# A gather and matmul stage: 704 gathered value columns, and dense value rows in pairs of blocks from block 32

## The reference

```python
    # xt: (256, 2048); idx, gate: (256, 8 heads, 16 experts); U, Vt: (16384, 2048)
        u = U[ib]
        hid = jax.nn.gelu(jnp.einsum('td,thkd->thk', xb, u))
        v = Vt[ib]
        return jnp.einsum('thk,thkd->td', gb * hid, v)
    x = x + peer_layer(h2, ...)
    return rms_norm(x, norm_f_g)
```

## Time and profile before

| | |
|---|---|
| median of 3 runs | 2129.06 us (2127.1 to 2131.72) |
| the profiled execution: time | 2132.88 us |
| its span, first to last instruction | 2131.1 us |
| mean granted clock of PE | 0.841 of full |
| value stage, about | 1612 to 2117 us of the span |
| PE busy | 1480.5 us (69%) |
| DVE busy | 1619.7 us (76%) |
| ACT busy | 872.1 us (41%) |
| POOL busy | 969.6 us (46%) |

### The profile page before, as it was taken

The page is one execution under the profiler, slowest core; times in us unless marked ns, Lnnn a source line. Parts: engine busy times, 40 slices in busy tenths (PEclk is TensorE's granted clock), DMA queues, the critical chain, the costliest instruction groups (busy, mean ns, idle before and its releaser), DMA issues.

```text
span 2131.1 us, 26457 instructions
## 1 busy us (share of the span) xinstructions
PE 1480.5 (69%) x9809; PEld 1371.6 (64%) x9809; DVE 1619.7 (76%) x2122; ACT 872.1 (41%) x1116; POOL 969.6 (46%) x699
## 2 busy tenths in 40 slices
PE   6999999999999999910000002211358999999997
PEld 6987998898999889910000002211347999999996
DVE  5465764545644556789999999877888999899997
ACT  4354432344333444211211226577655444444443
POOL 1002220000000000178888878888866776667763
PEclk9999999999999999965555555555589999999998
DMA  5555344434455554699999999999917999999996
GB/s 202 177 178 194 139 139 138 153 135 158 158 178 178 198 178 167 250 361 422 421 422 408 416 369 411 412 421 417 419 52 263 357 358 358 350 358 359 359 358 229
DMA packets 151818, 597.85 MB, mean 281 GB/s; under 512 B 14720, under 2 KB 14736, under 8 KB 118288
## 3 DMA queue, kind: packets, MB, share of 16 engines
q0 software_dynamic: 58048, 356.02, 42.0%
q1 hardware_dynamic: 93648, 240.22, 32.0%
HBM read 594.09 MB, written 2.10 MB: 280 GB/s over the span
## 4 chain that ended last, share of the span: by engine, by line
PE 47%; issue 20%; POOL 13%; DVE 13%; DMA 5%; ACT 1%; POOLq 0%; DVEq 0%; SPq 0%; ACTq 0%; PEldq 0%
PE acc L1608 8%; PE acc L1611 8%; PE acc L1610 8%; POOL slots L495 6%; POOL starts L534 5%; DVE slots L1397 5%; PE acc L1625 3%; PE acc L1627 3%; PE acc L1626 3%; DMA starts<-in_v_gather,expert 2%; DMA slots<-in_peer_u,expert 2%; PE acc L1922 2%; PE scr L1924 2%; PE acc L1924 2%; PE scr L1922 2%
## 5 line engine op out<-in xcount | busy, mean ns | idle before, releaser
L881 DVE TENSOR_TENSOR w_lo<-raw,w_hi 128x2048 fp32r<-128x2048 f32 x136 | 314.7, 2315 | 302.8 <-ACT w_hi L550 301.8
L1397 DVE SCALAR_TENSOR_TENSOR slots<-slots,acc 128x2048 f32<-128x2048 f32 x188 | 424.7, 2285 | 46.6 <-DMA slots<-in_peer_u,expert 44.4
L550 ACT ACTIVATE w_hi<-raw 128x2048 fp32r<-128x2048 f32 x136 | 260.1, 1913 | 428.7 <-PE acc L1611 286.5
L534 POOL DMA_INDIRECT starts<-in_v_gather,expert x256 | 343.8, 1343 | 158.9 <-issue 81.3
L495 POOL DMA_INDIRECT slots<-in_peer_u,expert x256 | 250.9, 980 | 260.6 <-DVE expert L1369 148.4
L1608 PE MATMUL acc<-hT_hi,w_hi 128*128 128x256 f32 x1024 | 294.6, 288 | 3.0 <-PE acc L1611 1.7
L503 POOL TENSOR_TENSOR slots<-slots,N 128x2048 f32<-128x2048 f32 x62 | 280.7, 4528 | 31.5 <-DMA slots<-in_peer_u,expert 31.2
L843 ACT ACTIVATE v_hi<-v_raw 128x1408 fp32r<-128x1408 f32 x128 | 177.0, 1384 | 284.3 <-PE scr L1924 213.1
L1610 PE MATMUL acc<-hT_lo,w_hi 128*128 128x256 f32 x1024 | 292.1, 285 | 0.0
L1611 PE MATMUL acc<-hT_hi,w_lo 128*128 128x256 f32 x1024 | 291.9, 285 | 0.0
L746 ACT ACTIVATE slots<-slots 128x2048 f32<-128x2048 f32 x62 | 118.4, 1910 | 366.7 <-POOL slots L503 366.7
(11 more groups left out here) (284 smaller groups left out, 3341.9 us busy)
## 6 DMA issues: line engine op xcount, KB each, us to landing
raw<-in_w_in SPq DMA_DIRECT2D x88, 1024.0 KB
v_raw<-in_v_dense SPq DMA_DIRECT2D x128, 704.0 KB
raw<-in_w_o SPq DMA_DIRECT2D x16, 1024.0 KB
raw<-in_peer_wq SPq DMA_DIRECT2D x16, 1024.0 KB
raw<-in_w_a_up SPq DMA_DIRECT2D x8, 1024.0 KB
raw<-in_w_b_up SPq DMA_DIRECT2D x8, 1024.0 KB
slots<-in_peer_u,expert POOLq DMA_INDIRECT x256, 9.2
starts<-in_v_gather,expert POOLq DMA_INDIRECT x256
```

The source lines that it names most:

```text
L534: pool.indirect_dma_start(starts[s % CRING][:, :], None, v_gather[:, :], bass.IndirectOffsetOnAxis(ap=expert[:, s // NSEL, s % NSEL:s % NS ...
L550: a.activation(w_hi[:, m % 2, :, :], raw[:, m % 2, :, :], ACT.Copy).then_inc(hi_ready, 1)
L881: v.tensor_tensor(w_lo[:, m % 2, :, :], raw[:, m % 2, :, :], w_hi[:, m % 2, :, :].bitcast(fp32), ALU.subtract).then_inc(lo_ready, 1)
L1397: v.scalar_tensor_tensor(out=slots[j][:, :], in0=slots[j][:, :], scalar=1.0, in1=row, op0=ALU.mult, op1=ALU.mult, accum_out=hid_sum[:, t, ...
```

## The change

CW goes from 640 to 704, so that gathers fetch 2816 B a row and the dense part has 1344 columns. Blocks 0 to 31 keep their form (halves of 768 and 576 columns, pieces of 512, 256, 256 and 320). From block 32 (PAIRED_FROM) on:

- SP loads two blocks with one DMA into one of three buffers `v_pair`, 128 x 2688 each. The first lies on SBUF space that `weight_of` for blocks 0 to 31 occupies, the third on that of two `v_raw` buffers; their loads wait accordingly. From the fourth pair on, a load waits until the low parts of the pair that held the buffer are made.
- DVE makes the low part of a block in one operation of 1344 columns, into one of two `v_lo` buffers, waiting for PE to be through with the block before the last (at block 32: with the last). Its two adds follow directly.
- PE waits for a whole block and does tile 0, then tile 1, each in three pieces of 512, 512 and 320 columns.

The core of the diff:

```diff
-CW = 640
+CW = 704
+VBANKS = ((0, 512), (512, 1024), (1024, DW))
+PAIRED_FROM = 32
+PAIRS = 3
@@ buffers
+        v_pair = [at(f"v_pair{j}", kib, [2, DW]) for j, kib in enumerate((24, 34.5, 112))]
-        v_hi, v_lo = at("v_hi", 184, [2, DW], f32r), at("v_lo", 160, [DW], f32r)
+        v_hi = at("v_hi", 184, [2, DW], f32r)
+        v_lo = [at(f"v_lo{n}", kib, [DW], f32r) for n, kib in enumerate((160, 105))]
@@ SP
+            for n in range(PAIRED_FROM, BLOCKS, 2):
+                j = (n - PAIRED_FROM) // 2
+                if j == 0:
+                    sp.wait_ge(e_ready, PAIRED_FROM // 2)
+                elif j == PAIRS - 1:
+                    sp.wait_ge(v_ready, 2 * PAIRED_FROM)
+                elif j >= PAIRS:
+                    sp.wait_ge(v_ready, 2 * (n - 2 * PAIRS) + 4)
+                sp.sem_inc(granted_w, 1)
+                sp.dma_start(v_pair[j % PAIRS][:, :, :], v_dense[:, n:n + 2, :]).then_inc(pair_landed[j % PAIRS], 16)
@@ DVE
+                else:
+                    if n == PAIRED_FROM:
+                        dve.wait_ge(v_used, 2 * n)
+                    elif n > PAIRED_FROM + 1:
+                        dve.wait_ge(v_used, 2 * (n - 2) + 2)
+                    v.tensor_tensor(v_lo[n % 2][:, :], raw_of(n)[:, :], v_hi[:, n % 2, :].bitcast(fp32),
+                                    ALU.subtract).then_inc(v_ready, 2)
+                    add_start(2 * n)
+                    add_start(2 * n + 1)
@@ DVE, after the last block
-                dve.wait_ge(first_done if t == 0 else v_used, 1 if t == 0 else 2 * BLOCKS)
+                dve.wait_ge(v_used, 2 * BLOCKS - 1 + t)
@@ PE
+                else:
+                    pe.wait_ge(v_ready, 2 * n + 2)
                     for t in range(NT):
+                        add(t, VBANKS, v_lo[n % 2]).then_inc(v_used, 1)
```

More of the change, by code:

```diff
@@ L240, in build @@
                      [weight_of1[:, q * P // PIECES:(q + 1) * P // PIECES, :] for q in range(PIECES)]]
-        v_raw = [at(f"v_raw{n}", kib, [DW]) for n, kib in enumerate((112, 117.5, 105))]
-        v_hi, v_lo = at("v_hi", 184, [2, DW], f32r), at("v_lo", 160, [DW], f32r)
+        v_raw = [at(f"v_raw{n}", kib, [DW]) for n, kib in enumerate((112, 117.25, 105))]
+        v_pair = [at(f"v_pair{j}", kib, [2, DW]) for j, kib in enumerate((24, 34.5, 112))]
+        v_hi = at("v_hi", 184, [2, DW], f32r)
+        v_lo = [at(f"v_lo{n}", kib, [DW], f32r) for n, kib in enumerate((160, 105))]
         e_hi, e_lo = at("e_hi", 97, [2, NT, 2 * P], f32r), at("e_lo", 101, [2, NT, 2 * P], f32r)
@@ L245, in build @@
         y_first = at("y_first", 128, [NT, CW])
-        starts = [at(f"starts{n}", kib, [CW]) for n, kib in enumerate((123, 125.5, 195, 197.5, 165.5))]
+        starts = [at(f"starts{n}", kib, [CW]) for n, kib in enumerate((122.5, 125.25, 194.5, 197.25, 165.25))]
         ff_room = at("ff_room", 200, [2 * KB])
@@ L355, in build, with raw_of @@
         v_landed = [sem(f"v_landed{j}") for j in range(RAWS)]
+        pair_landed = [sem(f"pair_landed{j}") for j in range(PAIRS)]
         e_hi_ready, e_ready, v_hi_ready, v_ready, v_used = (
             sem("e_hi_ready"), sem("e_ready"), sem("v_hi_ready"), sem("v_ready"), sem("v_used"))
-        first_done, first_gained, first_out = sem("first_done"), sem("first_gained"), sem("first_out")
+        first_gained, first_out = sem("first_gained"), sem("first_out")
         y_summed, y_ready, out_done = sem("y_summed"), sem("y_ready"), sem("out_done")
+        def raw_of(n):
+            return v_raw[n % RAWS] if n < PAIRED_FROM else v_pair[(n - PAIRED_FROM) // 2 % PAIRS][:, n % 2, :]
         block = ctx.enter_context(nc.Block())
@@ L411, in _ @@
             load_v(2)
-            for n in range(RAWS, BLOCKS):
+            for n in range(RAWS, PAIRED_FROM):
                 sp.wait_ge(v_ready, 2 * (n - RAWS) + 2)
@@ L839, in _ @@
             for n in range(BLOCKS):
-                act.wait_ge(v_landed[n % RAWS], 16 * (n // RAWS + 1))
+                if n < PAIRED_FROM:
+                    act.wait_ge(v_landed[n % RAWS], 16 * (n // RAWS + 1))
+                else:
+                    j = (n - PAIRED_FROM) // 2
+                    act.wait_ge(pair_landed[j % PAIRS], 16 * (j // PAIRS + 1))
                 if n >= 2:
                     act.wait_ge(v_used, 2 * (n - 2) + 2)
-                a.activation(v_hi[:, n % 2, :], v_raw[n % RAWS][:, :], ACT.Copy).then_inc(v_hi_ready, 1)
+                a.activation(v_hi[:, n % 2, :], raw_of(n)[:, :], ACT.Copy).then_inc(v_hi_ready, 1)
                 if n % 2 and n + 1 < BLOCKS:
@@ L1550, in _ @@
                 dve.wait_ge(v_hi_ready, n + 1)
[L1551 to L1556, removed]
+                if n < PAIRED_FROM:
+                    for c, cols in enumerate(VHALF):
+                        if n:
+                            dve.wait_ge(v_used, 2 * (n - 1) + c + 1)
+                        v.tensor_tensor(v_lo[0][:, cols], raw_of(n)[:, cols], v_hi[:, n % 2, cols].bitcast(fp32),
+                                        ALU.subtract).then_inc(v_ready, 1)
+                        add_start(2 * n + c)
+                else:
[7 more added lines that the diff above has]
+                    add_start(2 * n + 1)
                 if n % 2 and n + 1 < BLOCKS:
@@ L1913, in _, with add @@
                 e_cols = slice(n % 2 * P, (n % 2 + 1) * P)
-                for c in range(2):
-                    pe.wait_ge(v_ready, 2 * n + c + 1)
-                    for t in range(NT):
[L1917 to L1928, removed]
+                def add(t, pieces, low):
+                    flat = (acc, scr)[t][:, :, :].rearrange("p a n -> p (a n)")
+                    eh, el = e_hi[:, n // 2 % 2, t, e_cols], e_lo[:, n // 2 % 2, t, e_cols]
+                    for at0, end in pieces:
+                        to, cols = flat[:, at0:end], slice(at0, end)
+                        clear, stop = n == 0 and at0 % GW == 0, n == BLOCKS - 1
+                        t_.matmul(to, eh, v_hi[:, n % 2, cols], start=clear, stop=False, skip_group_check=True)
+                        t_.matmul(to, eh, low[:, cols], start=False, stop=False, skip_group_check=True)
+                        last = t_.matmul(to, el, v_hi[:, n % 2, cols], start=False, stop=stop, skip_group_check=True)
+                    return last
@@ L1931 @@
+                if n < PAIRED_FROM:
+                    for c in range(2):
+                        pe.wait_ge(v_ready, 2 * n + c + 1)
+                        for t in range(NT):
+                            last = add(t, VPIECES[c], v_lo[0])
+                        last.then_inc(v_used, 1)
+                else:
+                    pe.wait_ge(v_ready, 2 * n + 2)
+                    for t in range(NT):
+                        add(t, VBANKS, v_lo[n % 2]).then_inc(v_used, 1)
 _INS = ["x", "norm1_g", "w_in", "fox_f_bias", "hg_lb_logits", "hg_norm_g", "w_a_up", "w_b_up", "w_o", "norm2_g",
```

## The result

The changed kernel took 2152.55 us (median of 4 runs, 2150.45 to 2158.9) beside 2130.39 us for the kernel before (4 runs). The ratio is 1.0106, 95% interval 1.0085 to 1.0127: slower by 22 us. The forecast was 2135 us, range 2108 to 2149.

What follows compares the result with a forecast made beforehand. The prediction took PE to set the pace, at 3.86 us a block, with transfers just fast enough. Terms -4.8 + 8.6 + 3.3 - 1.0 = +6.1 us on a 2129.1 us median gave 2135 us, range 2108 to 2149.

Steps and rivals of the forecast that it cites:

- PE and DVE floors: From block 32, work per block without waits: PE 3.67 us, DVE 3.69 us, so a floor of about 3.68 us.
- Blocks 0 to 31: Fewer dense columns cut PE from 3.86 to 3.68 us a block; with a few adds waiting, -4.8 us.
- The gather ring: From block 32, bunched adds leave gathers less time to land; period 3.95 instead of 3.86 us over 96 blocks, +8.6 us.
- 2P = 0.76 + landing: From block 32, period P per block follows from a gather's landing time, counted from POOL's start; 7.15 us gives 3.95.
- the right side: The whole change was forecast slower, +6.1 us; chances were slower 0.46, same 0.20, faster 0.34.
- meeting a pair in flight: Gather packets each wait behind one longer dense packet; 0.2 us added to a usual landing.
- The seam: At block 32 the first pair's load waits for the low weights of blocks 30 and 31, idling PE: +3.3 us.
- The tail: In the last block DVE adds tile 0 under tile 1's 9 matmuls: -1.0 us.
- In time: Rival: gathers land within 6.6 us, so PE and DVE set 3.68 us a block; -19.8 us, 2109 us, chance 0.34.
- Rate as the bound: Rival: a transfer ceiling of 358 GB/s makes every block need 3.94 us; 2141 us, chance 0.06.

Runs made afterwards that it cites:

- run 9: 704 columns, single loads, seven gather and five dense buffers, plus two low buffers in halves from block 32: 2113.52 us, ratio 0.991 to the kernel before.
- run 2: The changed kernel with each pair loaded by two DMAs issued together, packets of 5376 B instead of 10752 B: 2149.73 us, ratio 1.0082 to the kernel before.
- run 11: The changed kernel with its six blocks of dense buffers each loaded by its own DMA once free: 2140.31 us, ratio 1.0036 to the kernel before.
- run 4: The changed kernel with single-block loads into three buffers, whole low parts and two adds together kept: 2135.85 us, ratio 1.0014 to the kernel before.
- Run 6: The changed kernel with a sixth gather buffer from gather 75 on: 2134.75 us, ratio 1.0006 to the kernel before.
- runs 1 and 6 to 9: Run 6, run 9 and three with 704 columns, single loads: five gather buffers, 2128.9 us; seven, 2122.44 us; seven plus five dense buffers, 2119.17 us.
- run 3: The changed kernel, pair loads kept, with low parts in halves and an add behind each: 2168.0 us, ratio 1.0174 to the kernel before.

## Why the prediction was wrong in size

*PE and DVE floors: right.* PE was to take 3.67 us for a block in three pieces and took 3.64 (1757.29 less 0.17 us of wait, from 1753.48); fewer matmuls brought nothing of their own.

```profile
1753.48 0.39 PE L1955 MATMUL acc<-v_hi,e_hi 128*128 128x512 f32 x1
...
1757.29 0.47 PE L1955 MATMUL acc<-v_hi,e_hi 128*128 128x512 f32 x1
```

DVE's two adds together are 2.00 us long, so the first steps 1.05 us where I had 0.98; its floor is 1.47 + 1.05 + 0.87 + 0.34 = 3.73 us instead of 3.69.

*Blocks 0 to 31: half.* -4.8 us was the term, about -2.4 came. Over the first blocks DVE and PE share one low buffer and take turns in waiting for each other, 3.77 us a block instead of 3.68; run 9, with two buffers, took some of that away later in the stage.

*The gather ring: the right term, mis-sized.* "[...] a usual landing which I put at 6.85, just at the quickest late one: 7.15 us, P = (0.76 + 7.15)/2 = 3.95" is the step that failed. The term was 8.6 us and measured 17.2. By the formula 2P = 0.76 + landing, the measured 4.123 us a block ask for a landing of 7.49 us where I had 7.15.

Two errors of opposite sign stand in that term. The pace after was forecast at 3.95 and is 4.123, over 96 blocks 16.6 us too low. The pace before was taken as PE's 3.86, but is 3.938 in this stretch with its waits, some 7.5 us too low over 96 blocks. Against 3.938 the forecast pace of 3.95 would have meant +1 us and the whole sum no change; that the forecast had the right side is in part luck.

The formula also uses one landing for all gathers, while the late ones cost the time. The trace has lost some of the semaphore updates that tell of landings; from those it kept, 12 of 16 a gather in the mean (14 before), I estimate a median landing of 7.1 us (6.6 before), and 8.7 us or more for one gather in ten (7.5 before). So the usual landing was near what I had put; its spread is what I left out. Of the 383.5 us from block 34 to 127, 347 are DVE's work, 93 x 3.73, 30.2 its waits for gathers, and the rest other waits. Checked at one place the formula is 3% off: with the gather of 7.52 us it gives 8.28 us for two blocks, where the pattern above took 8.03. I had allowed 0.2 us for meeting a pair in flight, reasoning on one dense packet ahead of each gather packet. What the runs show in its place: with short packets in the same burst (run 2) little of the loss is gone. With the same bytes, depth and compute form but single loads (run 11) two thirds of it are gone in time, 3.1 of 12.0 us of that at the seam, but the waits for gathers only fall from 30.2 to 27.3 us; with three blocks ahead instead of six (run 4) they fall to 22.0. So both the 1344 KB asked for at once and the larger amount asked for ahead seem to make gathers late; how much is due to each stays open. Run 6 shows from the other side that late gathers carry the loss.

The Trainium skill's rule from "DMA: Bandwidth & Descriptors" (queues, rings and completion order), that an engine finishes a packet before it turns to another queue, pointed to packet length; by run 2 its share is about 0.24% of the 1.06%, and by the intervals between nothing and half. The trace does not show how an engine chooses, nor whether the packets of that rule are the rows counted here, so why the pair loads hurt more than their packets stays open.

*The seam: right in kind.* 2.69 us of PE idle at block 32 where 3.3 were forecast; its timeline has

```profile
1736.69 0.31 PE L1957 MATMUL scr<-v_hi,e_lo 128*128 128x320 f32 x1
1739.69 0.76 PE L1955 MATMUL acc<-v_hi,e_hi 128*128 128x512 f32 x1 [2.69 <-DVE v_lo L1587]
```

but block 33's second add then waited 1.77 us for a gather (1745.56 above), behind two pairs requested at once; all in all 4.5 us. This wait was not in my sum; that the two pairs made that gather late is inferred from the order of the requests, and no run shows it by itself.

*The tail: wrong sign.* -1.0 us forecast, +0.3 measured. The second add starts at 2138.11, 1.2 us after the last matmul's start (2136.87), where before it was 1.4 (2118.15 and 2116.78): the add of tile 0 is queued behind the gain of the first columns, which waits for ACT's squares (2135.84), and so gets no cover from tile 1's matmuls. I had not looked at what stands ahead of it.

*Rivals.* "In time" did not come about in the changed kernel. Run 9 reaches 19 us under the kernel before, where 19.8 were forecast for that case, but with single loads, seven gather buffers and another form on DVE and PE, so the near number is a coincidence. "Rate as the bound" at 358 GB/s is refuted: 365 to 373 GB/s held for 350 us in runs 1 and 6 to 9. The Trainium skill, in the specifications of "DMA: Bandwidth & Descriptors", puts the HBM limit of a core at some 358 GB/s; these runs, with one core at work, disagree. Whether more than 373 GB/s can be held for as long, no run shows.

## What to carry to other kernels

A ring of buffers has a budget: uses per turn times the pace, less issue and a late landing, not the usual one. Write it down before moving consumers together or speeding up the pace, since both cut it, and add the buffer first. Here a load made twice as large, and more bytes asked for ahead, made the small transfers beside them later; where these have little slack, load the same bytes in even pieces, no further ahead than needed. And an experiment that splits an operation must be checked for the wait that the split itself brings (run 3).

## What the runs showed of the hardware beyond that

Length of packets hardly changed what a byte costs. In the changed kernel 10752 B packets took 43.9% of 350 us x 16 engines for 57.89 MB, 42.5 us of one engine's time a MB, and 5632 B packets before 50.2% for 64.15 MB, 43.8 us a MB; that is 3% more.

```profile
q1 hardware_dynamic: 6067, 57.89, 43.9%
```

```profile
q1 hardware_dynamic: 12810, 64.15, 50.2%
```

The engines' busy share is not a measure of their reserve: the kernel before moved 353 GB/s at a share of 0.96 in these 350 us, run 9 moved 372 at 0.97.
